# S5's gate on two PSUM pairs, its store by feature without a wait, and the recurrence's first operands released apart

## The reference, cut to what matters

```python
# end of the S5 branch (512 features, 640 tokens)
y = jax.nn.gelu(y)
y = y * jax.nn.sigmoid(y @ p['s5_w_glu'] + p['s5_b_glu'])
...
# RWKV-7 recurrence, for each direction, from r, decay, k, v, kk, b
def step(s, inp):
    r_t, w_t, k_t, v_t, kk_t, b_t = inp
    sa = jnp.einsum('bhvk,bhk->bhv', s, kk_t)
    s = s * w_t[:, :, None, :] - sa[..., None] * b_t[:, :, None, :] + v_t[..., None] * k_t[:, :, None, :]
    return s, jnp.einsum('bhvk,bhk->bhv', s, r_t)
```

## Time and profile before

| | |
|---|---|
| median of 3 runs | 2160.12 us (2158.44 to 2167.43) |
| the profiled execution | 2158.93 us, span of its instructions 2156.9 us |
| PE busy | 1928.3 us, 89% |
| DVE / ACT / POOL busy | 1016.9 / 494.8 / 690.6 us |
| end of S5: last transposes to the first instruction of the recurrence's phase | 554.0 to 589.7 us |
| opening of the recurrence: to PE's second level of unit 0 | 589.7 to 631.2 us |

### The profile page before, as it was taken

The page is one execution under the profiler, slowest core; times in us unless marked ns, Lnnn a source line. Parts: engine busy times, 40 slices in busy tenths (PEclk is TensorE's granted clock), DMA queues, the critical chain, the costliest instruction groups (busy, mean ns, idle before and its releaser), DMA issues. The chain is left out here.

```text
span 2156.9 us, 40487 instructions
## 1 busy us (share of the span) xinstructions
PE 1928.3 (89%) x15900; PEld 1420.2 (66%) x15900; DVE 1016.9 (47%) x2092; ACT 494.8 (23%) x936; POOL 690.6 (32%) x1036
## 2 busy tenths in 40 slices
PE   7999999897689999999999977998799999999966
PEld 2565645465467777777777766954577888877732
DVE  3867676566345435454454344646712222222228
ACT  2111132120233333333333322101121121211100
POOL 4526000000042324332342322322234444444435
PEclk9999999999899999999999998999899999999988
DMA  9234656562041211122111018630099989999955
GB/s 281 59 130 138 224 185 218 178 228 84 35 123 58 84 47 51 41 67 69 46 37 39 8 43 280 217 123 30 35 369 345 332 303 314 330 327 324 339 209 247
DMA packets 227871, 355.64 MB, mean 165 GB/s; under 512 B 38257, under 2 KB 156804, under 8 KB 223892
## 3 DMA queue, kind: packets, MB, share of 16 engines
q1 hardware_dynamic: 200926, 300.73, 40.8%
q0 software_dynamic: 24496, 45.01, 6.0%
q10 hardware_dynamic: 2310, 7.92, 1.0%
HBM read 307.11 MB, written 84.34 MB: 181 GB/s over the span
## 5 line engine op out<-in xcount | busy, mean ns | idle before, releaser
L2824 DVE TENSOR_TENSOR me_hh<-me_sg,ps_ju 128x128 f32<-128x128 f32 x76 | 21.9, 288 | 389.3 <-PE ps_jd L2776 372.7
L452 PE MATMUL ps_s<-hT,w_in_sb 128*128 128x512 f32 x432 | 196.3, 608 | 0.0
L2768 PE MATMUL ps_jg<-me_xT,me_wg 128*128 128x128 f32 x1216 | 152.1, 279 | 0.0
L1346 PE MATMUL ps_gs<-hT,gt_w 128*128 128x512 f32 x256 | 143.4, 643 | 7.3 <-PEq L76 7.3
L2768 PE MATMUL ps_ju<-me_xT,me_wu 128*128 128x128 f32 x1216 | 148.6, 275 | 0.0
L2768 PEld LDWEIGHTS ps_jg<-me_xT,me_wg 128*128 128x128 f32 x1216 | 145.5, 196 | 0.0
L2776 PE MATMUL ps_jd<-me_wd,me_hh 128*128 128x512 f32 x304 | 143.1, 593 | 2.4 <-DVE me_yb L2830 2.4
L452 PEld LDWEIGHTS ps_s<-hT,w_in_sb 128*128 128x128 f32 x432 | 82.3, 196 | 94.5 <-issue 93.9
L2768 PEld LDWEIGHTS ps_ju<-me_xT,me_wu 128*128 128x128 f32 x1216 | 142.5, 193 | 0.0
L2045 POOL TENSOR_TENSOR rc_lj<-rc_l,rc_lev 128x256 f32<-128x256 f32 x100 | 74.2, 762 | 177.9 <-PE ps_c L1737 177.7
L2797 ACT ACTIVATE me_xT<-ps_jx 128x1024 f32<-128x1024 f32 x77 | 78.9, 1025 | 210.5 <-PE ps_jx L2759 210.5
(11 more groups left out here) (564 smaller groups left out, 3971.9 us busy)
## 6 DMA issues: line engine op xcount, KB each, us to landing
me_wg<-in_exp_w_gate SPq DMA_DIRECT2D x76, 512.0 KB
me_wu<-in_exp_w_up SPq DMA_DIRECT2D x76, 512.0 KB
me_wd<-in_exp_w_down SPq DMA_DIRECT2D x76, 512.0 KB
w_ad_sb<-in_w_ada SPq DMA_DIRECT2D x32, 512.0 KB
w_in_sb<-in_w_in SPq DMA_DIRECT2D x31, 512.0 KB
gt_w<-in_w_in SPq DMA_DIRECT2D x24, 512.0 KB, 4.4
cb_rows<-yj_dram SPq DMA_DIRECT2D x6, 2048.0 KB
zr<-in_w_ada SPq DMA_DIRECT2D x4, 2048.0 KB, 9.3
```

Of the source, the lines that this page charges most:

```text
L452: mm(ps_s[:, b, :], w_in[:, r, k, :], hT[:, k, 0:TS], start=(k == 0), stop=(k == KT - 1))
L1346: nc.tensor.matmul(ps_s[:], w[:, t % WR, k, :], hT[:, k, 0:TS], start=(k == 0), stop=(k == KT - 1))
L2768: last = mm(o[:, 0:P], w[:, s, k, :], xT[:, s % 2, k, :], start=(k == 0), stop=(k == KT - 1))
```

## The change

It has five edits.

- The gated unit's blocks use `ps_gate[f % 2]`, so two PSUM pairs in turn. Block 1 waits for `s_f5_sb` = 8 (DVE has read `ps_u` for the last time), block f >= 2 for ACT's sigmoid of f-2. In block 0 the wait for gelu goes with each k instead of for all four ahead of it.
- `yc` is stored by feature block as soon as that one is multiplied, and the phase doesn't wait for the landings. `s_sp5` is allocated directly, outside `phase_sems`; the load of `vt` into `yc`'s memory waits for all four.
- `sig` has a semaphore of its own, `c_sg`, and DVE's scans wait for that alone; POOL's `hats` waits for the other four loads.
- POOL's order in `hats` becomes `ah`, `bh` (signal `c_ab`), `kh`, `rh`, `rkd` (signal `c_stage`). PE's first two products of a unit wait for `c_ab`, the third for `c_stage`.
- `RF_PAD`, an empty tile under `ya` in `rwkv_finish`, grows from 3456 to 7552 floats for each partition: `ya` lies 16 KB higher.

```diff
             def _(sp):
                 sp.dma_start(glu_w, a["s5_w_glu"].rearrange("(k p) n -> p k n", p=P)).then_inc(m.s_glu_w, 16)
-                sp.wait_ge(m.s_yc5, MT)
-                sp.dma_start(m.y_dram[2], yc[:]).then_inc(m.s_sp5, 16)
-                sp.wait_ge(m.s_sp5, 16)
+                for f in range(MT):
+                    sp.wait_ge(m.s_yc5, f + 1)
+                    sp.dma_start(m.y_dram[2, :, f], yc[:, f]).then_inc(m.s_sp5, 16)
...
                 pe.wait_ge(m.s_glu_w, 16)
-                pe.wait_ge(m.s_ge5, MT)
                 pe.wait_ge(m.s_fin_sb, 1)
                 for f in range(MT):
-                    if f:
-                        pe.wait_ge(m.s_glu_sb, f)
+                    if f == 1:
+                        pe.wait_ge(m.s_f5_sb, 2 * MT)
+                    if f >= 2:
+                        pe.wait_ge(m.s_glu_sb, f - 1)
                     for b, sl in ((0, slice(0, TS)), (1, slice(TS, N))):
                         for k in range(MT):
-                            last = nc.tensor.matmul(ps_g[:, b, 0:sl.stop - sl.start], glu_w[:, k, f * P:(f + 1) * P], y_f[:, k, sl],
+                            if f == 0 and b == 0:
+                                pe.wait_ge(m.s_ge5, k + 1)
+                            last = nc.tensor.matmul(ps_gate[f % 2][:, b, 0:sl.stop - sl.start], glu_w[:, k, f * P:(f + 1) * P], y_f[:, k, sl],
                                                     start=(k == 0), stop=(k == MT - 1))
                     last.then_inc(m.s_glu_mm, 1)
...
-RF_PAD = 3456
+RF_PAD = 7552
...
                     for buf, u in ((sig, U_SIG + n % 2), (r_in, U_R), (kk, U_KK), (kd, U_KD + n % 2), (bd, U_BD + n % 2)):
-                        sp.dma_start(buf[:], m.u_dram[u, :, :, t]).then_inc(m.c_in, 16)
+                        sp.dma_start(buf[:], m.u_dram[u, :, :, t]).then_inc(m.c_sg if buf is sig else m.c_in, 16)
                 load(0)
                 fill(FILL_START)
                 load(1)
+                sp.wait_ge(m.s_sp5, 16 * MT)
                 sp.dma_start(m.vt[:], m.vtok_dram.rearrange("t p c -> p t c")).then_inc(m.c_vt, 16)
...
                 for n in range(UNITS):
                     d = n % 2
-                    pe.wait_ge(m.c_stage, n + 1)
+                    pe.wait_ge(m.c_ab, n + 1)
...
                         if k == 2:
                             fill(FILL_GRAM)
+                            pe.wait_ge(m.c_stage, n + 1)
                             pe.wait_ge(m.c_L, n * 3 + 3)
...
                 def scans(n):
 
-                    dve.wait_ge(m.c_in, 80 * (n + 1))
+                    dve.wait_ge(m.c_sg, 16 * (n + 1))
...
-                    pool.wait_ge(m.c_in, 80 * (n + 1))
+                    pool.wait_ge(m.c_in, 64 * (n + 1))
...
-                    G.tensor_tensor(rkd[:], r_in[:], kd[:], ALU.mult)
+                    G.tensor_tensor(ah[:, d], kk[:], ex[:, 2], ALU.mult)
+                    G.tensor_tensor(bh[:], bd[:], ex[:, 1], ALU.mult).then_inc(m.c_ab, 1)
+                    G.tensor_tensor(kh[:], kd[:], ex[:, 1], ALU.mult)
                     G.tensor_tensor(rh[:, d], r_in[:], ex[:, 0], ALU.mult)
-                    G.tensor_tensor(ah[:, d], kk[:], ex[:, 2], ALU.mult)
-                    G.tensor_tensor(kh[:], kd[:], ex[:, 1], ALU.mult)
-                    G.tensor_tensor(bh[:], bd[:], ex[:, 1], ALU.mult).then_inc(m.c_stage, 1)
+                    G.tensor_tensor(rkd[:], r_in[:], kd[:], ALU.mult).then_inc(m.c_stage, 1)
...
+            m.s_sp5 = nc.alloc_semaphore("s_sp5")
             s5_scan(nc, m, a)
```

More of the change, by code:

```diff
@@ L986, in s5_scan @@
         (m.s_la0, m.s_la1, m.s_la2, m.s_la3, m.s_lt, m.s_u_mm, m.s_u_sb, m.s_zz_mm, m.s_zz_sb, m.s_x5, m.s_y5_mm, m.s_y5_sb, m.s_f5_mm, m.s_f5_sb,
-         m.s_ge5, m.s_glu_mm, m.s_glu_sb, m.s_glu_w, m.s_out5, m.s_fin_mm, m.s_fin_sb, m.s_du5, m.s_sp5, m.s_yc5, m.s_ut_mm,
+         m.s_ge5, m.s_glu_mm, m.s_glu_sb, m.s_glu_w, m.s_out5, m.s_fin_mm, m.s_fin_sb, m.s_du5, m.s_yc5, m.s_ut_mm,
          m.s_ut_sb, m.s_wt_sb) = sems(
             nc, m, "s_la0 s_la1 s_la2 s_la3 s_lt s_u_mm s_u_sb s_zz_mm s_zz_sb s_x5 s_y5_mm s_y5_sb s_f5_mm s_f5_sb s_ge5 s_glu_mm s_glu_sb "
-            "s_glu_w s_out5 s_fin_mm s_fin_sb s_du5 s_sp5 s_yc5 s_ut_mm s_ut_sb s_wt_sb")
+            "s_glu_w s_out5 s_fin_mm s_fin_sb s_du5 s_yc5 s_ut_mm s_ut_sb s_wt_sb")
         def pb(name, shape):
@@ L1257, in _ @@
                     act.wait_ge(m.s_glu_mm, f + 1)
-                    nc.scalar.activation(yc[:, f, 0:TS], ps_g[:, 0, :], ACT.Sigmoid, bias=m.pcol[:, b0 + f:b0 + f + 1])
-                    nc.scalar.activation(yc[:, f, TS:N], ps_g[:, 1, 0:TP], ACT.Sigmoid,
+                    nc.scalar.activation(yc[:, f, 0:TS], ps_gate[f % 2][:, 0, :], ACT.Sigmoid, bias=m.pcol[:, b0 + f:b0 + f + 1])
+                    nc.scalar.activation(yc[:, f, TS:N], ps_gate[f % 2][:, 1, 0:TP], ACT.Sigmoid,
                                          bias=m.pcol[:, b0 + f:b0 + f + 1]).then_inc(m.s_glu_sb, 1)
 GT = 3 * D // P
-RF_PAD = 3456
+RF_PAD = 7552
 GT_S5 = 8
@@ L1624, in rwkv_units @@
         s_ps = bank[1]
-        (m.c_vt, m.c_in, m.c_one, m.c_cs, m.c_d, m.c_ex, m.c_stage, m.c_gr, m.c_L, m.c_gd, m.c_y1, m.c_xd, m.c_x1, m.c_lj, m.c_g,
+        (m.c_vt, m.c_sg, m.c_ab, m.c_in, m.c_one, m.c_cs, m.c_d, m.c_ex, m.c_stage, m.c_gr, m.c_L, m.c_gd, m.c_y1, m.c_xd, m.c_x1, m.c_lj, m.c_g,
          m.c_gsb, m.c_yg, m.c_xg, m.c_yup, m.c_xup, m.c_kb_mm, m.c_kb, m.c_bo_mm, m.c_bo, m.c_stz, m.c_sts, m.c_rh_mm,
@@ L1628, in rwkv_units @@
          m.c_var, m.c_pow, m.c_nrm, m.c_gn) = sems(
-            nc, m, "c_vt c_in c_one c_cs c_d c_ex c_stage c_gr c_L c_gd c_y1 c_xd c_x1 c_lj c_g c_gsb c_yg c_xg c_yup c_xup "
+            nc, m, "c_vt c_sg c_ab c_in c_one c_cs c_d c_ex c_stage c_gr c_L c_gd c_y1 c_xd c_x1 c_lj c_g c_gsb c_yg c_xg c_yup c_xup "
             "c_kb_mm c_kb c_bo_mm c_bo c_stz c_sts c_rh_mm c_rh c_u_mm c_un c_y_mm c_y c_s_mm c_s c_st c_sum c_mu c_yc "
```

## The result

The changed kernel took 2145.18 us in the median (2142.14 to 2154.67, 6 runs) beside 2160.08 (2158.44 to 2167.43, 6 runs) of the kernel before: a ratio of 0.9929, 95% interval 0.9908 to 0.9951, 0.7% faster. The forecast was 2145. The profiled execution has a span of 2142.3 us, 14.6 less than before.

The account below looks back on a forecast made before the run. The prediction took PE, busy 89% of 2156.9 us, as the bound and priced its gaps ahead of barriers: 3.9 + 3.8 + 4.1 + 2.5 = 14.3 us off, giving 2145 us. The range was 2138.5 to 2151.5.

Parts of the forecast that it names:

- Part 1: Gated unit's block 0: starting without the last gelu and an earlier return of PE's clock end it 3.9 us earlier.
- three cases: Earlier clock returns in the trace, 4.4, 4.3 and 3.4 to 3.5 us after dense work began, used to time block 0.
- The bounds: Block 0's gain range: 4.5 us if the clock is back at 557.5, 1.3 if it stays at half.
- Part 2: Gated unit's blocks 1 to 3: the second PSUM pair removes PE's wait for ACT, 3.8 us; other bound 3.1.
- Rival (c): Gated unit: the second PSUM pair is worth nothing; 10.5 us in all, 2149.5 us; chance 0.04.
- Part 3: Phase border after the store: only the last quarter's issue and barriers remain; gain 4.1 us, or 0 if a landing is awaited.
- Rival (d): Store at the phase's end: the last quarter's landing is still awaited, 3 us or so; 2148.5 us; chance 0.06.
- Part 4: Unit 0's scans: DVE starts once `sig` lands, and everything up to `c_stage` moves 3.2 us earlier.
- Part 5: Hats' order in unit 0: third products 8.0 us earlier, clipped by `at_rev` and lost clock; net 2.5 us with the scans.
- Rival (a): Recurrence's opening: the `load(1)` chain doesn't end last, so the full 8 us arrive; total 19.8, 2140 us; chance 0.13.
- Sum: All edits together: 3.9 + 3.8 + 4.1 + 2.5 = 14.3 us, for a forecast of 2145 us.
- Rival (e): Recurrence: new PE stops bring half clock, 1.8 us each; at 14 extra spells 11 us slower, 2171; chance 0.04.

Follow-up runs that it names:

- the third profile: The changed kernel unaltered, profiled a third time; `at_rev` landed 1.0 us later and level 3 came 44.75 us after the phase's start.
- the first profile: The changed kernel's original profiled execution, with a span of 2142.3 us; level 3 came 42.60 us after the phase's start.
- the bias row ahead: Changed kernel with unit 0's bias row prepared before the hats, written and `at_rev` loaded before `load(1)`; medians 2148.83, 2144.32 and 2139.56 us.
- one pair: Changed kernel with the gated unit's four blocks back in one pair of banks, each gelu's wait kept; 2149.06 us, ratio 0.9949.
- all gelus awaited: Changed kernel with block 0 of the gated unit waiting for all four gelus, pairs kept; one run of 2145.37 us.

## Why the prediction was right

- **Part 1, block 0: 3.9 forecast, 3.5 measured** (ACT's first sigmoid 8.12 us after the last transposes, 565.63 - 554.04 = 11.59 before). The clock's return was set too early: it was back at about 566.5, 5.05 us after the block's start and 6.1 after the transposes, not 4.7, and so later than any of the three cases (3.4 to 4.4 us) that it was taken from. The bounds held it.
- **Part 2, the pair: 3.8 forecast**, 3.9 in the row of blocks and 3.9 by taking the pair away. Rival (c) is out.
- **Part 3, the store: 4.1 forecast, 4.1 measured** (5.42 to 1.35). Rival (d) is out. Had the landing of the last quarter been left, it would have cost 1.8 us, not the 3 of the rival.
- **Part 4: `c_stage` 3.2 us earlier forecast, 3.2 measured** (POOL's first hat at 9.06 us after the phase's start, 12.25 before). PE's first product came at 11.64 for 11.5, `load(1)`'s first issue 15.31 us after the phase's start (599.92) for 15.3. The masks behind `at_rev` started 3.9 us earlier, not 3.2; in the third profile it is 2.9, so the difference lies within the landing's own scatter of 1 us.
- **Part 5: 8.0 us at the third set forecast, 8.2 measured; a stop of 5 us at level 2, 4.42 measured; 4.3 left there, 5.1 measured; 1.8 lost to the clock, 1.4 measured; net 2.5 forecast, 3.7 measured (1.6 in the third profile).** The mechanism was the one named, with both its terms a little oversized. One step leaned on more than it said: PE came to the first product without a stop only because its gate tile began at half clock, as in the kernel before. With full clock there, as in two of the experiments, it stopped for 2.65 us and the third set came 1.5 us later. Rival (a), the full 8 us, is out in the changed kernel, and what it would need, the wait for `at_rev` gone, was made and gave 9.1 us at level 3 (46.34 to 37.2).
- **Sum: 14.3 forecast, 15.2 in the edits' own stretches, 14.6 in the spans, 14.9 in the medians.** That the last two are so close is in part chance: 6.3 us more ahead of S5's end and 5.1 less behind level 3 nearly cancel, and by the third profile the edits' own stretches give 13.1. `RF_PAD`'s 0 was not tested by itself. Over all executions the means are 2162.2 (43 runs) and 2144.2 (19 runs), 18.0 us with a standard error of 1.4: more than the edits' 15.2, and the shorter recurrence of the changed kernel's profiles is the place where the rest can lie.
- **Rival (e)** named the mechanism that moves the totals, and sized one spell of half clock at 1.8 us (1.6 and 3.3 at the two places above). It took only new stops of PE for its cause; but old stops gain and lose spells too, and in the first profile this went for the change. The prediction's sentence that a gain ahead of a barrier moves all that follows, unless a wait takes it back, leaves this out: of the 5.4 us that the bias row ahead gave back, a longer wait of PE was 0.6 and the clock the rest.

## What to carry to other kernels

When a step is released earlier, list what else hangs on the same signal and does not move: here one bias row behind a load on SP's queue took back 4.5 of 8.2 us. Price each edit by the anchors right before and behind it (the same instruction in both timelines), and don't take a later stretch of the same instructions for constant: with PE stops in it, its length changed by up to 10 us here though PE's own program in it was the same. Look there for what the edit has moved on the other engines too. And an edit's worth depends on the edit beside it: the order of the hats was worth at most 0.8 us, or 5.2.

## What the runs showed of the hardware

- TensorE's granted clock makes the length of unchanged code vary. Behind level 3 of unit 0 the same PE instructions took 644.76 and 644.83 us in two executions of the changed kernel, 650.13 and 650.14 in two with the bias row ahead, and 654.54 where the store was waited for.
- A stop's length alone didn't tell whether the clock was lost. A stop of 2.64 us was met with half clock in all fourteen profiles. One of 1.71 us came with half clock in seven of them and without it in seven. Behind the stop of 3.2 us at the phase's border nine profiles had half clock and two (one pair, all gelus awaited) had full.
- The same four DVE scans took 2.71 us in one execution and 3.90 in another, where POOL's masks started 0.6 us sooner beside them.
- A store of a quarter of 1280 KB cost 1.8 us of waiting behind its issue, the whole 4.1.
